# Output projection of a hybrid decoder step: the first slab with the contraction slice outermost over six token tiles

## What is computed

```python
mix = jnp.concatenate([o_a * jax.nn.silu(gate_a), o_s * jax.nn.silu(gate_s), o_m * jax.nn.silu(gate_m)], axis=-1)
y = x + mix @ w_out          # mix: 1056 tokens x 2048, w_out: 2048 x 2048
y = rmsnorm(y, g_final)
```

## Time and profile before

| | us |
|---|---|
| median of three runs (2048.11, 2048.57, 2054.72) | 2048.57 |
| profiled execution, its own time | 2051.07 |
| span of the profiled execution | 2049.5 |
| TensorE busy | 1854.8 (91%) |
| VectorE busy | 1093.5 (53%) |
| ScalarE busy | 839.8 (41%) |
| output projection, first to last matmul | 1650.1 to 2036.3 |

### The profile page before, as it was taken

One profiled execution on the slowest core, in us unless ns is written; L12 is line 12 of the kernel. 1 busy time (PEld: TensorE's weight loads), 2 busy tenths in 40 slices (PEclk: granted clock), 3 DMA queues, 4 the chain that ended last, 5 costly groups with the idle time before them and its releaser, 6 DMA issues. The chain is left out here.

```text
span 2049.5 us, 31740 instructions
## 1 busy us (share of the span) xinstructions
PE 1854.8 (91%) x12954; PEld 1265.3 (62%) x12954; DVE 1093.5 (53%) x2056; ACT 839.8 (41%) x1447; POOL 293.8 (14%) x182
## 2 busy tenths in 40 slices
PE   6979999999999999999999797898887359898997
PEld 4555555556666666666666456565554148787886
DVE  5543145559876876777846026765545562122225
ACT  5454467663333433344323024543345153233431
POOL 3022211111211211112111000220022040000000
PEclk9989999999999999999999899999999569999999
DMA  8422211112222223222220631101037012222224
GB/s 328 139 73 73 67 48 57 43 63 74 91 73 85 70 75 93 70 84 74 91 73 36 240 131 61 32 21 57 1 107 248 20 63 63 64 63 64 63 74 180
DMA packets 187096, 175.93 MB, mean 86 GB/s; under 512 B 27526, under 2 KB 168486, under 8 KB 184198
## 3 DMA queue, kind: packets, MB, share of 16 engines
q1 hardware_dynamic: 166742, 133.18, 20.7%
q10 hardware_dynamic: 14640, 22.96, 3.0%
q0 software_dynamic: 5568, 17.72, 2.5%
HBM read 139.66 MB, written 34.17 MB: 85 GB/s over the span
## 5 line engine op out<-in xcount | busy, mean ns | idle before, releaser
L659 PE MATMUL ps<-h,w 128*128 128x352 f16 (+2 forms) x6096 | 947.8, 316 | 6.4 <-POOL w L932 6.1
L659 PEld LDWEIGHTS ps<-h,w 128*128 128x128 f16 (+1 forms) x6096 | 597.1, 99 | 340.1 <-issue 15.3
L2155 PE MATMUL ps<-w_f,m 128*128 128x256 f16 x3072 | 349.4, 277 | 35.1 <-POOL w_f L2094 16.7
L2155 PEld LDWEIGHTS ps<-w_f,m 128*128 128x128 f16 x3072 | 303.9, 99 | 79.0 <-POOL w_f L2094 17.8
L932 POOL TENSOR_TENSOR w<-wb,w 128x2048 f16<-128x2048 f32 (+1 forms) x45 | 186.6, 4148 | 845.3 <-ACT w L791 845.3
L799 ACT ACTIVATE zst<-ps,unit 128x352 f32<-128x352 f32 (+1 forms) x112 | 63.3, 577 | 317.2 <-PE ps L659 293.1
L1131 DVE MAX8 m<-score 128x8 f32<-128x1024 f32 (+2 forms) x192 | 171.6, 894 | 5.7
L2220 DVE SCALAR_TENSOR_TENSOR y_room<-ps,unit_f,x_f 128x256 f32 (+1 forms) x64 | 31.0, 484 | 266.4 <-PE ps L2155 242.1
L1132 DVE MATCH_REPLACE8 score<-m,score 128x1024 f32<-128x1024 f32 (+2 forms) x192 | 168.1, 876 | 0.0
L1123 DVE SCALAR_TENSOR_TENSOR score<-room,wis,score 128x1024 f32<-128x1024 f32 (+5 forms) x90 | 92.3, 1026 | 79.4 <-ACT room L854 74.3
L787 ACT ACTIVATE wb<-wb,unit 128x2048 f32<-128x2048 f32 (+1 forms) x45 | 89.5, 1988 | 90.5 <-DVE unit L946 90.5
(11 more groups left out here) (414 smaller groups left out, 1775.6 us busy)
## 6 DMA issues: line engine op xcount, KB each, us to landing
wb<-in_w_in_dram SPq DMA_DIRECT2D x44, 1024.0 KB, 5.2
z_scratch<-zst ACTq DMA_DIRECT2D x32, 528.0 KB, 2.6
score<-in_w_out_dram SPq DMA_DIRECT2D x8, 2048.0 KB, 11.6
y_room<-z_scratch SPq DMA_DIRECT2D x8, 1056.0 KB, 17.5
x_in<-in_x_prompt_dram SPq DMA_DIRECT2D x8, 1024.0 KB, 6.9
w_kv<-in_w_mem_kv_dram POOLq DMA_DIRECT2D x16, 512.0 KB, 4.9
x_f<-in_x_prompt_dram SPq DMA_DIRECT2D x8, 1024.0 KB, 5.4
out_y_p_dram<-y_room SPq DMA_DIRECT2D x8, 1024.0 KB, 3.9
```

Of the source, the lines that this page charges most:

```text
L659: last = nc.tensor.matmul(ps[0:m, n, 0:w], w16[:, b, pw_, k, 0:m], h16[:, ph, k, t0:t0 + w], start=(k == 0 and i == 0), stop=(k == KT - 1 ...
L2155: last = nc.tensor.matmul(ps[:, bank(b, t), 0:SLAB], m16[:, mp, k, t * P:(t + 1) * P], w16[:, b, wp, k, :], start=(k == 0 and j == 0), sto ...
```

## The change

The PE code of slab 0 is written out by itself and in another order. A new function `slab_by_depth` takes the slices k outermost: for each k it waits as before for the weights' quarter and for the slice of the activations, and then does the three matmuls of that slice for each of the first six tiles, which lie in the six banks of the ring. After it the sum of sizes for slab 1 is computed. Then tiles 6, 7 and the sample tile of slab 0 follow tile by tile, through `slab_products` with a range of tiles, then slab 1 as straight code. The hardware loop of TensorE now runs over slabs 2 to 5 (two rounds), and slabs 6 and 7 follow as before. The waits for `m_low` in the loop are gone, and `slab_by_depth` has no wait for free banks. The other engines' code is the same, their loops too.

```diff
-            def slab_products(s, b, more=True):
+            def slab_products(s, b, tiles=range(TILES_F), more=True):
-                for t in range(TILES_F):
+                for t in tiles:
                     pe.wait_ge(banks_free, TILES_F * s + (t + 1))
@@
                     for k in range(KT):
                         if t == 0 and k % 4 == 0:
                             pe.wait_ge(w_split, 4 * s + (k // 4 + 1))
-                        if t == 0 and b == 0:
-                            pe.wait_ge(m_low, k + 1)
@@
-            with pe.Fori(0, NSLAB // 2 - 1) as it:
+            def slab_by_depth():
+                for k in range(KT):
+                    if k % 4 == 0:
+                        pe.wait_ge(w_split, k // 4 + 1)
+                    pe.wait_ge(m_low, k + 1)
+                    for t in range(RING):
+                        for j, (mp, wp) in enumerate(((0, 0), (0, 1), (1, 0))):
+                            last = nc.tensor.matmul(ps[:, bank(0, t), 0:SLAB], m16[:, mp, k, t * P:(t + 1) * P], w16[:, 0, wp, k, :],
+                                                    start=(k == 0 and j == 0), stop=(k == KT - 1 and j == 2))
+                        if k == KT - 1:
+                            last.then_inc(y_mm, 1)
+                sum_sizes(1, 1)
+
+            slab_by_depth()
+            slab_products(0, 0, range(RING, TILES_F))
+            slab_products(1, 1)
+            with pe.Fori(1, NSLAB // 2 - 1) as it:
                 for b in range(2):
                     slab_products(it * 2 + b, b)
             slab_products(NSLAB - 2, 0)
```

## The result

The changed kernel takes 2021.78 us, median of four runs (2016.87 to 2031.78), against 2048.34 for the kernel before in the same comparison: ratio 0.987, 95% interval 0.984 to 0.989. It is 26.6 us faster. Forecast were 2025.1 us within 2017 to 2036.

The account below looks back on a forecast made before the run. TensorE was taken to bound the output projection, nearly alone. From the profiled 2051.1 us, 13.0 for slab 0's order and 10.5 for one loop return gave 2027.6, or 2025.1 against the median; range 2017 to 2036.

Parts of the forecast that it names:

- Part 1: Slab 0's first six tiles run without further waits while slices arrive: 31.7 us plus 2.1 us for the low starting clock.
- Part 2: New 3.7 us wait before slab 1's sum of sizes, for ScalarE's pass; slab 0 still gains 13.0 us.
- I take no fall: In the new wait before slab 1's sum of sizes, the granted clock was assumed not to fall, costing nothing.
- the bound of 2.1: Range allowance at the new wait in slab 0: 2.1 us less gain if the clock falls there.
- Part 3: Slab 1's weights, prepared later against TensorE, still come in time: cost nothing, slack 0.6 us, otherwise up to 2.3 us a quarter.
- Part 4: PE loop over slabs 2 to 5: the return after slab 1 goes, gaining 10.5 us; that after slab 3 stays at 7.7.
- the loop's entry: TensorE's entry into the loop ahead of slab 2, new on the path: taken as nothing, at most 10.5 us.
- Rival (b): Code moves in memory and the remaining return finds its head at hand: 7.7 us more gained, 2017.4 us; 8%.
- the prediction's own signs: Listed signs of being wrong: gaps in the 288 matmuls, clock 0.50 beyond 10 us, gap before slab 2, last gap another size.
- (a): Entering the loop ahead of slab 2 costs a gap as a return did: 10.5 us back, 2035.6 us; 15%.
- (c): Changing the bank every three matmuls keeps the clock low in the six tiles: 6.9 us slower than before, 2055.5 us; 4%.
- (d): TensorE is not the bound; DMA of slab 2's or later weights takes the gain back: within 0.3% of before; 3%.

Follow-up runs that it names:

- the filler: The changed kernel with 32 full spare matmuls into unused bank 6, in the wait before slab 1's sum of sizes; stage 366.9 us, 6.7 less than the changed kernel.
- the kernel with the order alone: The changed kernel, but with a PE loop of three rounds over slabs 1 to 6, so two returns again; stage 377.0 us, ratio 0.988 against the kernel before.
- the shifted kernels: The changed kernel with 18, 32 or 64 single-column spare matmuls ahead of the first product; stages 378.5, 368.7 and 376.2 us against 373.6.
- seven useless matmuls: The kernel before with 7 single-column spare matmuls (14 instructions) ahead of the PE loop, nothing else changed; stage 381.3 us against 399.4.
- the one with 64 spare matmuls: The changed kernel with 64 single-column spare matmuls (128 instructions) ahead of the first product; stage 376.2 us against 373.6.

## Why the prediction was right, point by point

**Part 1 held.** No wait within the six tiles; 33.12 us against 31.7 + 2.1 = 33.8. The lower clock at the start cost 1.4 us here (1.2 to 2.7 us over the kernels with this order), where I took 2.1.

**Part 2: the wait held, the clock didn't.** Its working gave 3.7 us and it was 3.51, released by ScalarE's pass as named. The step that failed is "I take no fall": the clock fell and cost 1.7 us. It lay within the bound of 2.1, and the filler showed it for certain. The trace of before couldn't decide it, and that of after shows why one can't argue it from the length alone: the wait of 3.5 us cost clock in the changed kernel, a gap of 3.50 us cost none in the kernel with the order alone, and one of 3.40 us cost 1.5 there. So slab 0 took 50.6 us and not 49.8.

**Part 3 held.** Slab 1's last low half ended 3.4 us after the slab's start, as before, and TensorE didn't wait. That its slack was small came out when the sum came 1.4 us later and, without the wait, slab 0 ended 5.6 us sooner.

**Part 4: right in the sum, incomplete in its reason.** The gap after slab 1 went (10.5 us), the loop's entry cost nothing, as the rows of VectorE's entry and of the exit had suggested. The return after slab 3, left at 7.7 us, cost 4.8. That term was mis-sized because it was treated as a property of the loop; it is one of the head's place in the code, as the shifted kernels showed: 0, 4.8 to 5.1, and 9.5 us for one and the same loop. Rival (b) named the place of the code, gave it 8% and priced it at all or nothing. The return did get cheaper, by 2.9 us, and the shifts speak for the code's place as the reason, though the head still wasn't at hand. By the prediction's own signs the last gap at another size speaks against this term. What makes one return of the kernel before 2.8 us dearer than the other (10.5 against 7.7), with the head at one and the same place, is open: in the dearer one the second packet of code came 6.1 us after the first and not 3.1, with the DMA engines at 0.98 from 1761 to 1762 against 0.28 from 1857 to 1858; no run tests whether the other loads held it up.

The terms together: forecast -13.0 and -10.5, measured -12.3, -10.5 and -2.9. The clock behind the wait cost 1.7 us that the sum left out; the start cost 0.7 us less than it took, the wait 0.2 less and the return 2.9 less. These errors have opposite signs, so that the stage came out only 2.3 us below the forecast, which is luck in part. The remaining 1 us of the 3.3 between forecast and median is within what the stages ahead vary by.

**The rivals.** (a) is refuted by slab 2 at 1735.68. (c) is refuted: the bank changes every three matmuls and 288 of them keep the clock at 1.00 from the start's low stretch on. (d) is refuted: the sums of sizes in slabs 1 to 6 never waited.

## What to carry to other kernels

Where an engine's inputs come slice by slice, put as many outputs side by side as the slices' rate asks for, and no more: four or five tiles were enough here, and the sixth made the first result, on which another engine's long pass hung, end too late. Follow the first and the last result of a reordered block separately, and whatever is queued behind each. And before a gain or a loss at a loop is put down to an edit, see where the loop's head now lies in the code: seven useless matmuls gained 18 us, two thirds of what the whole change did.

## What the runs showed of the hardware

- A TensorE loop of some 1,780 instructions returned free of charge or at 3.0 to 9.0 us idle with up to 2.1 us of lower clock behind it. Moving nothing but its head by 36, 64 and 128 instructions gave 9.5, 0 and 5.1 us in place of 4.8. A return that cost time went with 9 packets of code, a free one with none.
- Announcing the branch removed both gaps (9.02 and 5.62 us) and made the loop's exit pay a pause of 2.06 us. It brought no code ahead: the packet of the block behind the loop stayed away, and the loop's own code didn't come again.
- Changing the PSUM bank every three matmuls cost nothing: 288 matmuls of 256 columns took 33.12 us with the low clock at their start, and from 1646 to 1674.6 the clock was 1.00, at the 0.110 us each that they take in one bank.
- The granted clock stood at full through an idle stretch of 3.5 us and fell after it, with the engine already at work for some 0.6 us; gaps of 3.4 to 3.5 us cost from nothing to 1.7 us.
- The same code ahead of the stage took 1640 to 1654 us over 14 profiles. Measured from its first product the same code differed less between kernels: slab 0 took 62.8 to 63.2 us in the four with the old order, and the 288 matmuls 32.9 to 33.4 us in all with six tiles but the one with 64 spare matmuls (34.43). That was enough to tell a return of 4.8 us from a free one in a single run.
